# Mixer of a hybrid SSD / GLA / MoE layer: the router's shift product behind the first scores, and in the second step the output product of tile 0 ahead of the state-space product of tile 1

## The reference, cut to what matters

```
y = rmsnorm((ysl_f + ysl_b + d_skip * x_heads) * silu(z), ssd_norm_g)      # state-space heads, 512 wide
o = rmsnorm(gol_f + gol_b, gla_norm_g) * silu(g_out)                       # gated linear attention, 512 wide
x = x + m_lat[2] * (concat([y, o], -1) @ w_out)                            # output product, gated residual
h2 = rmsnorm(x, norm2_g) * (1 + m_lat[4]) + m_lat[3]                       # scale and shift
s = sigmoid(h2 @ w_router)                                                 # then group-limited top 2 of 32 experts
```

## Time and profile before

| | |
|---|---|
| time before, median of 3 runs | 2380.34 us (2379.8 to 2381.73) |
| the profiled execution | 2379.42 us, of which the span of the profile is 2377.7 us |
| PE busy | 2166.9 us, 91% of the span |
| DVE busy | 1637.9 us, 69% |
| ACT busy | 1137.4 us, 48% |
| mixer | about 898 to 1301 us |

### The profile page before, as it was taken

The page is one execution under the profiler, slowest core; times in us unless marked ns, Lnnn a source line. Parts: engine busy times, 40 slices in busy tenths (PEclk is TensorE's granted clock), DMA queues, the critical chain, the costliest instruction groups (busy, mean ns, idle before and its releaser), DMA issues. The chain is left out here.

```text
span 2377.7 us, 36401 instructions
## 1 busy us (share of the span) xinstructions
PE 2166.9 (91%) x11761; PEld 1711.5 (72%) x11761; DVE 1637.9 (69%) x2101; ACT 1137.4 (48%) x1477; POOL 512.4 (22%) x535
## 2 busy tenths in 40 slices
PE   4999999999899997999997389999999999999980
PEld 2776777777677776888886277787877878878760
DVE  1333333333677667777772889999999999999983
ACT  0222222222555552333332067777777777777763
POOL 1000000000001003233231023333332334334332
PEclk7999999999999996999998699999999999999995
DMA  8223334331598869998873637469978779899957
GB/s 323 67 67 118 117 113 140 119 127 56 182 332 304 293 211 316 315 309 288 301 254 73 233 88 235 129 215 291 327 237 273 222 242 374 273 318 316 373 170 296
DMA packets 208013, 537.25 MB, mean 226 GB/s; under 512 B 14768, under 2 KB 45483, under 8 KB 201387
## 3 DMA queue, kind: packets, MB, share of 16 engines
q1 hardware_dynamic: 174904, 424.71, 49.9%
q0 software_dynamic: 30512, 102.77, 16.5%
q10 hardware_dynamic: 2499, 8.45, 0.9%
HBM read 402.28 MB, written 133.61 MB: 225 GB/s over the span
## 5 line engine op out<-in xcount | busy, mean ns | idle before, releaser
L2180 ACT ACTIVATE w_hi_e<-w_gates 128x2048 fp32r (+1 forms) x103 | 197.9, 1923 | 212.3 <-issue 103.4
L2306 DVE TENSOR_TENSOR w_lo_e<-w_gates,w_hi_e 128x2048 fp32r<-128x2048 f32 x103 | 236.4, 2296 | 33.9 <-ACT w_hi_e L2180 33.9
L2306 DVE TENSOR_TENSOR w_lo_e<-w_ups,w_hi_e 128x2048 fp32r<-128x2048 f32 x102 | 233.3, 2288 | 35.8 <-ACT w_hi_e L2180 35.8
L2306 DVE TENSOR_TENSOR w_lo_e<-w_downs,w_hi_e 128x2048 fp32r<-128x2048 f32 x100 | 228.4, 2284 | 0.0
L2180 ACT ACTIVATE w_hi_e<-w_ups 128x2048 fp32r (+1 forms) x102 | 195.7, 1919 | 23.7 <-PE pd_e L2253 22.5
L2180 ACT ACTIVATE w_hi_e<-w_downs 128x2048 fp32r x100 | 191.6, 1916 | 0.7
L614 PE MATMUL pf<-raws,w_in_sb 128*128 128x256 f32 x800 | 179.0, 387 | 1.1 <-DVE raws L695 1.1
L2253 PE MATMUL pg_e<-w_hi_e,x_hi_e 128*128 128x512 f32 x408 | 167.1, 409 | 7.4 <-DVE w_lo_e L2306 7.4
L614 PEld LDWEIGHTS pf<-raws,w_in_sb 128*128 128x128 f32 x800 | 155.2, 195 | 23.4 <-DVE raws L695 1.5
L2158 POOL DMA_INDIRECT x_mid<-yb_e,to_e x50 | 127.5, 2551 | 187.2 <-DVE yb_e L2350 185.0
L2253 PE MATMUL pd_e<-w_hi_e,h_hi_e 128*128 128x512 f32 x400 | 162.2, 406 | 0.0
(11 more groups left out here) (429 smaller groups left out, 4711.1 us busy)
## 6 DMA issues: line engine op xcount, KB each, us to landing
w_gates<-in_w_gate_dram SPq DMA_DIRECT2D x32, 2048.0 KB, 12.0
w_ups<-in_w_up_dram SPq DMA_DIRECT2D x32, 2048.0 KB
w_downs<-in_w_down_dram SPq DMA_DIRECT2D x32, 2048.0 KB
w_mod_half<-in_w_mod_dram SPq DMA_DIRECT2D x16, 1024.0 KB, 6.6
abc_m<-a_rows SPq DMA_DIRECT2D x16, 1024.0 KB, 4.8
recs<-tok_rec SPq DMA_DIRECT2D x15, 968.0 KB, 7.8
qk_rec<-qk SPq DMA_DIRECT2D x14, 1024.0 KB, 3.9
qk<-qk_rec SPq DMA_DIRECT2D x14, 1024.0 KB
```

The lines of the kernel that those rows point to most:

```text
L2180: act.activation(w_hi[:, s % 3:s % 3 + 1, :], raw(part, half, place), ACT.Copy).then_inc(hi_done, 1)
L2306: dve.tensor_tensor(w_lo[:, s % 3:s % 3 + 1, :], raw(part, half, place), w_hi[:, s % 3:s % 3 + 1, :].bitcast(F32), ALU.subtract).then_inc( ...
```

## The change

Four edits, all in the mixer:
- The shift product goes from `at` to `tr`, loses its wait for the mask of tile 0, and is issued in step 0 between `attn(0)` and `ssd(0)` instead of after `gla(0)`.
- The first transposes, `turned_m(0, n)`, wait for the copy of the shift product (`shift_done`), since they write `tr`; `attn` of the later tiles no longer does.
- DVE's copy of it comes ahead of the loop, behind the decayed C of tile 0, instead of behind the gate of o in step 0.
- In step 1 alone PE's order becomes `attn(1)`, `turned_m(0)`, `project(0)`, `ssd(1)`, `gla(1)`. All other steps keep theirs. The lists of ACT, POOL and SP are as before.

```diff
             def router_shift():
                 pe.wait_ge(setup, 32)
-                pe.wait_ge(am_done, 2)
                 for k in range(KT):
-                    mm = pe.matmul(at[:, 0, 0:NE], mod[:, 3 * KT + k, 0:1].to_broadcast([P, P]), w_rt[:, k, :], start=(k == 0), stop=(k == KT - 1))
+                    mm = pe.matmul(tr[:, 0, 0:NE], mod[:, 3 * KT + k, 0:1].to_broadcast([P, P]), w_rt[:, k, :], start=(k == 0), stop=(k == KT - 1))
                 mm.then_inc(shift_ps, 1)
 
             def turned_m(t, n):
                 pe.wait_ge(o_done if n else y_done, t + 1)
                 if t:
                     pe.wait_ge(x_added, 2 * (t - 1) + n + 1)
+                else:
+                    pe.wait_ge(shift_done, 1)
...
                 if t:
                     pe.wait_ge(am_done, 2 * t)
-                    pe.wait_ge(shift_done, 1)
...
                     attn(now)
-                    ssd(now)
+                    if n == 0:
+                        router_shift()
+                    if n != 1:
+                        ssd(now)
                 if before is not None:
                     turned_m(before, 0)
                     turned_m(before, 1)
+                if n == 1:
+                    project(before, range(KT))
+                    ssd(now)
                 if now is not None:
                     gla(now)
-                if n == 0:
-                    router_shift()
                 if done is not None:
                     turned_x(done)
-                if before is not None:
+                if before is not None and n != 1:
                     project(before, range(KT))
...
             def router_shift():
                 dve.wait_ge(shift_ps, 1)
-                dve.tensor_copy(rt_shift[:, :], at[:, 0, 0:NE]).then_inc(shift_done, 1)
+                dve.tensor_copy(rt_shift[:, :], tr[:, 0, 0:NE]).then_inc(shift_done, 1)
                 dve.wait_ge(shift_done, 1)
...
             decayed_c(0)
+            router_shift()
             for n in range(LT + 2):
...
                     gated_o(now)
-                if n == 0:
-                    router_shift()
```

## The result

The changed kernel is slower: 2393.71 us median (2388.91 to 2396.51) against 2379.8 us for the kernel before on the same chips (2376.27 to 2381.73), a ratio of 1.0057 with a 95% interval of 1.0045 to 1.0069. That is +13.9 us. The profiled executions differ by 2391.9 - 2377.7 = +14.2 us of span. The forecast was 2396.3 us, +16.

The account below looks back on a forecast made before the run. PE was taken to bound the mixer, busy 22.00 of 22.00 us. DVE's +13.2 and a second clock fall gave +15.7, taken as +16.0: 2379.42 + 16.0 = 2395.4, plus 0.9 for the median, 2396.3 us; range 2390 to 2402.

Parts of the forecast that it names:

- the forecast's own case: Whole kernel: late start of tile 1's output product makes it +14 to +18 us slower; chance 0.62.
- rival 1: Output product of tile 0: weights do not set its start, everything 3.2 us sooner, +12.8, 2393 us; chance 0.12.
- a clock that is soon back: PE in step 2: clock high again soon after 969.3, transposes done before DVE's 977.9, result near +13.2 instead of +16.0.
- Step 1: Shift product, 3.62 us, fits the 4.21 us hole at no cost; alone worth up to 4.5 us.
- Step 2: Output product of tile 0 waits for its weights and starts at 943.2, only 2.7 us earlier; PE stands from about 932.
- Step 3: Output product of tile 0: 10 matmuls at the low clock, 38 at the high, 13.3 us, ending at 956.5.
- Step 4: DVE queue from sum of y to decayed C takes 10.08 us; residual sum of tile 0 starts +13.2 us later.
- Step 5: PE in step 2: a 5 us hole drops the clock; state-space product 7.22 us, tile 1's output product at 983.7.
- The account of who is to blame: DVE's sum of y waits for tile 1's late state-space product, delaying the residual sum; PE's chain ends 978.3, DVE's 977.9.
- Rival 2: Chain behind the output product is slower: decayed C takes 12.55 or clock stays low longer, +18.5 to +23; chance 0.16.
- Rival 3: Output product raises the clock, so tile 1's state-space and gated products run high: -7, 2373 us; chance 0.05.
- Rival 4: No change: the delay is real but steps from 3 on have room to take it in; chance 0.05.

Follow-up runs that it names:

- the gated product alone: Shift product in its new place; in step 1 only tile 1's gated product behind tile 0's output product, against the kernel before: 1.0046.
- the last of the combined runs: Changed kernel plus residual sum of tile 0 moved ahead, 12 idle products in step 2 and 34 in the first hole; against the kernel before: 1.0048.

## Why the prediction was right

The forecast was +16.0, the measured change +13.9 and the range of 2390 to 2402 us held it. By the number alone the forecast's own case (+14 to +18) is missed by a hair, and +13.9 lies nearer to rival 1's +12.8 and to the +13.2 for a clock that is soon back. The traces decide for the forecast's mechanism: the weights released the product at 943.45, and the clock was at 0.50 from 969 to 975. Point by point:

- **Step 1, the shift product is free and its gain is lost.** Right: it fits the hole, and the new order alone costs what the whole change costs. The copy stayed hidden and the scores of tile 1 started early. What I had not seen is that without the new order its gain is stopped sooner, by the decayed scores and decayed C of tile 1.
- **Step 2, the weights set the start.** Right, with the release named by the trace. That 943.45 meets the forecast of 943.2 so closely is luck: the last load was issued 1.1 us sooner than before (913.74 against 914.86) and took 29.6 us instead of 28.3, and over the seven traces in which PE waited for the weights the start went from 941.2 to 944.2. PE stood 14.3 us, not the 11 forecast, as it was through its transposes at 929.1. With fewer loads the low halves set it, as the same step said.
- **Step 3, the product takes 13.3 us.** 12.55 measured (943.45 to 956.00): the low clock lasted 2.7 us of it (to the row at 946.15), not 4.3. In the other executions that waited for the weights it took 12.7 to 13.8, so the term is right within its scatter.
- **Step 4, 10.08 us from the sum of y to the end of decayed C.** 968.74 + 1.21 - 959.87 = 10.08 us, to the hundredth. The residual sum moved by 12.55 against a forecast of 13.2.
- **Step 5, the second fall of the clock.** It came, in a hole of 5.48 us (forecast 5), the state-space product took 976.09 - 968.87 = 7.22 us, and the gated product started at 977.85 against 978.3. From there to the output product of tile 1 it took 4.35 us instead of the 5.4 that I had summed at the low clock: the clock rose on the way, the case for which I had said that up to 0.9 comes off. My terms added up to 983.7, and 982.20 was measured: this part is 1.1 us of the 1.5, and 0.4 had come off before it, step 3 above all. The other 0.6 us of the 2.1 are the 16.0 that I took where the sum gave 15.7, and the difference between spans and medians.
- **The account of who is to blame** was incomplete, without harm to the number. It had both chains into the gated product of tile 2, PE's a little the longer, and the runs bear that out. But it put DVE's delay on the sum of y behind the state-space product alone. The runs show two products that hold DVE: the gated product behind the output product is enough for 11.4 us, the state-space product adds 5.3.
- **Rivals.** The early weights (rival 1) are what the run with half the loads made on purpose. It took 3.2 us off the start, as that rival said; the pair with half the loads differs by 10.3 us instead of 13.9, which fits but is not clear of the noise. Rival 2 (a slower chain) did not come: decayed C took the 10.08. Rival 3 (faster) failed where it was said to, at the start of the product. Rival 4 (taken in later): steps from 3 on were 22.25 to 22.29 us in both kernels; only the last step, 1.2 us shorter after the change, took something in.

What stays open is how much of the 14 us the clock costs by itself. The run with the clock at 1.00 from 937 to 980 gained 6.3 us up to the output product of tile 1, but it also had the residual sum moved, and the late loads with the clock's next fall took all but 1.0 back. The difference between medians and spans in the run with the gated product alone (12.4 and 7.8 us) also stays; its interval of 1.0029 to 1.0063 is 6.9 to 15.0 us.

## What to carry to other kernels

Before a long product is moved ahead of short ones on an in-order engine, ask what waits for the short ones: here two short products fed a vector engine's queue, whose last entry was the one that consumes the long product. Ask also what the long product itself waits for; it had been hidden by the short ones and became a hole of 14 us. A single edit that shortens one of two equal chains shows nothing, so test them together before calling either harmless. And what both together win can be lost again at the next wait: the time of a whole execution did not show any of these gains.

## What the runs showed of the hardware

- The granted clock fell in a hole of only 2.31 us (the shift alone, 0.50 in the window 964 to 966) and in one of 2.43 us (the last of the combined runs, 0.50 from 1000 to 1003), while a hole of 1.33 us in the kernel before left it at 1.00. It also fell with hardly any idle time: the kernel with 12 idle products in step 2 had PE busy for 4.63 of 5 and 2.00 of 2 us and was at 0.80 from 972 to 974. The same 12 products held it in two other runs (1.00 from 965 to 973 and from 970 to 974) and failed in a third (0.50 from 970 to 974).
- The Trainium skill (TensorE: Matmul & The Clock Gate, "Why this matters for your kernels") advises to keep TensorE busy and to avoid idle gaps. The hole of 5.48 us and the fall in it (0.77 from 964 to 969) agree with that; a busy engine was no safeguard here, in the run above and in the 6.00 of 6.00 us at 0.50 after the change.
- The last of the output weights landed at 941.2 to 944.2 us in the seven traces in which PE waited for them, 46.9 to 48.6 us behind the block's first product (894.2 to 897.2), with the DMA queues at a share of 1.0 and some 410 GB/s. The landing moved with the entry into the block, within 1.7 us.
